# Channel layer norms: the next product takes x shifted by a pivot, and mean and deviation are applied when it is evicted

## What is computed

```python
def layer_norm(x, g, b):
    mu = x32.mean(-1, keepdims=True)
    var = jnp.square(x32 - mu).mean(-1, keepdims=True)
    return ((x32 - mu) * lax.rsqrt(var + LN_EPS) * g + b)

xp = ffn_sublayer(xp, ffn1_w_gu, ffn1_w_down, ln_g[0], ln_b[0])   # layer_norm(ALPHA*x + 0.5*swiglu(x))
qa, ka, va, qr, kr, vr, gr, ga, gb = split_inputs(xp, w_in)
oa = diff_post(diff_attention_prompt(qa, ka, va, lam), ...)
ob = ret_post(retention_prompt(qr, kr, vr), gr)
xp = merge_sublayer(xp, oa, ob, ga, gb, w_pa, w_pb, w_o, ln_g[1], ln_b[1])
xp = ffn_sublayer(xp, ffn2_w_gu, ffn2_w_down, ln_g[2], ln_b[2])
```

## Time and profile before

| | us |
|---|---|
| median of three runs (1946.41 to 1950.22) | 1946.93 |
| span of the profiled execution (the page gives its span, no other time of it) | 1943.7 |
| busy: PE, DVE, ACT, POOL | 1804.9, 778.9, 667.4, 85.2 |

### The profile page before, as it was taken

The page is one execution under the profiler, slowest core; times in us unless marked ns, Lnnn a source line. Parts: engine busy times, 40 slices in busy tenths (PEclk is TensorE's granted clock), DMA queues, the critical chain, the costliest instruction groups (busy, mean ns, idle before and its releaser), DMA issues.

```text
span 1943.7 us, 33105 instructions
## 1 busy us (share of the span) xinstructions
PE 1804.9 (93%) x13247; PEld 1699.9 (87%) x13247; DVE 778.9 (40%) x1081; ACT 667.4 (34%) x899; POOL 85.2 (4%) x113
## 2 busy tenths in 40 slices
PE   6999999998997768999989999999999899999996
PEld 5999999987997537878768999869998799999996
DVE  2333332234223875756663223344345433333123
ACT  3333331124223555666563222124322433332111
POOL 0000000000002420000000000110000000000002
PEclk9999999999997998999989999999999999999998
DMA  4222222230440015767752232062223022222221
GB/s 142 91 90 91 89 84 82 81 108 22 133 133 23 1 51 176 273 228 249 242 169 91 87 98 84 17 215 66 91 91 100 22 86 87 89 90 84 92 97 46
DMA packets 146659, 203.75 MB, mean 105 GB/s; under 512 B 5538, under 2 KB 127330, under 8 KB 146594
## 3 DMA queue, kind: packets, MB, share of 16 engines
q1 hardware_dynamic: 145442, 198.35, 31.4%
q0 software_dynamic: 1152, 4.46, 0.6%
HBM read 191.39 MB, written 11.40 MB: 104 GB/s over the span
## 4 chain that ended last, share of the span: by engine, by line
PE 88%; DVE 4%; ACT 4%; issue 2%; DMA 0%; SPq 0%; POOL 0%; ACTq 0%; POOLq 0%; DVEq 0%
PE ps L297 68%; PE ps L1201 4%; PE ps L1232 3%; PE ps L1187 2%; PE ps L974 1%; PE ps L988 1%; PE ps L614 1%; PE ps L1624 1%; PE ps L1211 1%; PE ps L1616 1%; PE ps L1248 1%; PE ps L699 1%; PE ps L1198 1%; ACT aT L1069 1%; PE ps L981 0%
## 5 line engine op out<-in xcount | busy, mean ns | idle before, releaser
L297 PE MATMUL ps<-xh,w_hi_t 128*128 128x272 f32 x2432 | 510.1, 291 | 25.3 <-DVE xl L651 18.3
L297 PE MATMUL ps<-xh,w_lo_t 128*128 128x272 f32 x2432 | 505.9, 290 | 0.0
L297 PE MATMUL ps<-xl,w_hi_t 128*128 128x272 f32 x2432 | 504.2, 289 | 0.0
L283 DVE TENSOR_TENSOR w_lo_t<-w_raw,w_hi_t 128x2048 fp32r<-128x2048 f32 (+1 forms) x112 | 252.4, 2254 | 519.2 <-ACT w_hi_t L279 519.2
L297 PEld LDWEIGHTS ps<-xh,w_hi_t 128*128 128x128 f32 x2432 | 385.0, 190 | 30.2 <-issue 20.7
L297 PEld LDWEIGHTS ps<-xl,w_hi_t 128*128 128x128 f32 x2432 | 385.1, 190 | 0.0
L297 PEld LDWEIGHTS ps<-xh,w_lo_t 128*128 128x128 f32 x2432 | 382.4, 190 | 0.0
L279 ACT CAST w_hi_t<-w_raw 128x2048 fp32r<-128x2048 f32 (+1 forms) x112 | 209.9, 1874 | 276.5 <-PE ps L297 276.5
L297 PE MATMUL ps<-hh,w_lo_t 128*128 128x272 f32 x704 | 145.7, 288 | 0.0
L297 PE MATMUL ps<-hh,w_hi_t 128*128 128x272 f32 x704 | 145.5, 288 | 0.0
L297 PE MATMUL ps<-hl,w_hi_t 128*128 128x272 f32 x704 | 145.1, 288 | 0.0
(11 more groups left out here) (245 smaller groups left out, 2107.0 us busy)
## 6 DMA issues: line engine op xcount, KB each, us to landing
w_raw<-in_ffn_w_gu_dram SPq DMA_DIRECT2D x44, 1024.0 KB, 5.1
w_raw<-in_w_in_dram SPq DMA_DIRECT2D x32, 1024.0 KB, 5.7
k_page<-in_cache_k_dram SPq DMA_DIRECT2D x64, 512.0 KB, 4.8
v_page<-in_cache_v_dram SPq DMA_DIRECT2D x64, 512.0 KB, 4.6
w_raw<-in_ffn_w_down_dram SPq DMA_DIRECT2D x16, 1024.0 KB, 5.1
w_raw<-in_ffn_w_down_dram SPq DMA_DIRECT2D x8, 768.0 KB, 4.7
w_raw<-in_w_branch_a_dram SPq DMA_DIRECT2D x4, 1024.0 KB, 5.2
st_in<-in_state_ret_dram SPq DMA_DIRECT2D x8, 512.0 KB, 5.0
```

Of the source, the lines that this page charges most:

```text
L283: nc.vector.tensor_tensor(w_lo_t[:, j, 0:nk], w_raw[:, j, 0:nk], w_hi_t[:, j, 0:nk].bitcast(F32), ALU.subtract).then_inc(lo_split, 1)
L297: mm = nc.tensor.matmul(ps[:, bank + half, 0:HALF], w[:, j, k, w_cols], m[:, k0 + k, half * HALF:half * HALF + HALF], start=start and k == ...
```

## The change

What goes into the next product is no longer the normalised x. With a pivot c for each token (the mean of the first 256 channels), x - c is formed early; `xh` and `xl` get g * (x - c), and two more columns, -g and b, stand behind the 544 tokens. The product then holds W'g(x - c) and, in the two columns, -W'g and W'b. Mean and deviation of x - c come later, and the eviction computes (product + mean * (-W'g)) / deviation + W'b, in three DVE instructions (`dve_fix`) and the bias of the ACT instruction that evicts anyway. So:

- **Pivot.** When two of the 8 tiles are done, DVE adds them, PE multiplies by ones (`pe_pivot`, behind the first chunk of the second pair in the down projection and behind tile 2 of the output projection), ACT scales, and DVE adds -c to all 8 tiles of `xT`, the six that still lack their product among them (`dve_pivot`).
- **Each tile** is then squared and multiplied by g on ACT (`act_take`), the squares are added up on POOL in `x_ssq`, and DVE adds `x_sum` and makes the low part. `x_sq` is a single buffer.
- **The sums** over channels of `x_sum` and `x_ssq` are made by PE inside the next product's first tile, between its fifth and sixth k step (`between`, `pe_stats`).
- **Normalised x** is still needed: by the value projection after the first norm and from round 1 on in FFN 2. POOL subtracts the mean, DVE scales, ACT adds the bias and makes `xh`, DVE `xl`, all between the evictions of the product that took the raw x. `xh` is overwritten k by k behind that product's last tile (`freed`).
- `NormedProject` replaces `Project` for the key projection (all 8 tiles on raw x); in FFN 2 only round 0 is on raw x and stands written out ahead of the loop. The loops of the down projections and of the output projection are written out on PE, and on all three engines for the output projection.

The diff, cut to its core:

```diff
-        def gemm(bank, j, n, nk, mh_, ml_, k0=0, start=True, stop=True, tile_ready=None):
+        def gemm(bank, j, n, nk, mh_, ml_, k0=0, start=True, stop=True, tile_ready=None, extra=0, freed=None,
+                 between=None):
             for k in range(nk):
+                if between and k == 5:
+                    between()
                 if tile_ready:
                     tile_ready(k)
                 w_cols = slice(n * P, n * P + P)
                 for pas, (w, m) in enumerate(((w_hi_t, mh_), (w_hi_t, ml_), (w_lo_t, mh_))):
                     for half in range(2):
-                        mm = nc.tensor.matmul(ps[:, bank + half, 0:HALF], w[:, j, k, w_cols],
-                                              m[:, k0 + k, half * HALF:half * HALF + HALF],
+                        cols = HALF + extra * half
+                        mm = nc.tensor.matmul(ps[:, bank + half, 0:cols], w[:, j, k, w_cols],
+                                              m[:, k0 + k, half * HALF:half * HALF + cols],
                                               start=start and k == 0 and pas == 0,
                                               stop=stop and k == nk - 1 and pas == 2)
+                if freed and k < nk - 1:
+                    mm.then_inc(freed, 1)
             mm.then_inc(gemm_done, 1)
         def tile_done(eng, c, n):
...
+            def pe_up(self, pe, i, tile_ready=None, folded=None):
                 c = self.c
-                with pe.Fori(0, KF // 2) as i:
-                    for j in range(2):
-                        chunk_ready(pe, c + 2 * i + j)
-                        for n in range(2):
-
-                            pe.wait_ge(self.prod_done if j else self.silu_done, self.h0 + 2 * i + n + 1)
-                            gemm(4 * j + 2 * n, j, n, KD, xh, xl, tile_ready=None if j or n else tile_ready)
+                for j in range(2):
+                    chunk_ready(pe, c + 2 * i + j)
+                    for n in range(2):
+                        pe.wait_ge(self.prod_done if j else self.silu_done, self.h0 + 2 * i + n + 1)
+                        if folded and j:
+                            folded.sums_read(pe, n)
+                        first = j == 0 and n == 0
+                        gemm(4 * j + 2 * n, j, n, KD, xh, xl, tile_ready=tile_ready if first else None,
+                             extra=2 if folded else 0, freed=folded.freed if folded and j and n else None,
+                             between=(lambda: folded.pe_stats(pe)) if folded and first else None)
...
+                if folded:
+                    self.pe_up(pe, 0, lambda k: folded.raw_ready(pe, k), folded)
+                with pe.Fori(1 if folded else 0, KF // 2) as i:
...
+                for q in range(2):
...
+                                if norm and q == 1 and r == 0 and s == 0 and n == 0:
+                                    norm.pivot_kept(pe)
...
+                            if norm and q == 0 and m == 3:
+                                norm.pe_pivot(pe)
...
+            def dve_up(self, dve, i, folded=None):
                 c = self.c
-                with dve.Fori(0, KF // 2) as i:
-                    split_lo(dve, c + 2 * i + 2, 0)
+                if folded:
                     for n in range(2):
+                        folded.dve_fix(dve, n, c, n, 2 * n)
+                split_lo(dve, c + 2 * i + 2, 0)
+                if folded:
+                    for k in range(KD):
+                        folded.dve_scale(dve, k)
+                for n in range(2):
...
+                    if folded and n == 0:
+                        for k in range(KD):
+                            folded.dve_low(dve, k)
+                split_lo(dve, c + 2 * i + 3, 1)
...
+                ln2.dve_columns(dve)
+                for k in range(KD):
+                    c = self.c + k // 2
+                    tile_done(dve, c, k % 2)
+                    if k > 2:
+                        ln2.dve_shifted(dve)
+                    nc.vector.scalar_tensor_tensor(halves(xT[:, k]), banks(2 * (k % 4)), 1.0 / ALPHA, halves(xT[:, k]),
+                                                   ALU.mult, ALU.add).then_inc(self.resid, 1)
+                    if k == 2:
+                        dve.wait_ge(self.resid, k + 5)
+                        ln2.dve_pivot(dve)
+                        ln2.dve_raw_low(dve, 0)
+                        ln2.dve_raw_low(dve, 1)
+                    ln2.dve_take(dve, k, self.resid, 0)
+                    if k % 2 == 1:
+                        split_lo(dve, c + 2, k // 2 % 2)
+                ln2.dve_stats(dve)
```

More of the change, by code:

```diff
@@ L379, in act_part @@
+            def act_part(self, act, folded=None, norm=None):
+                c = self.c
+                if folded:
+                    self.act_up(act, 0, folded)
+                with act.Fori(1 if folded else 0, KF // 2) as i:
+                    self.act_up(act, i)
                 c += FFN_UP
+                if norm:
+                    norm.act_columns(act)
                 for q in range(2):
@@ L384, in act_part @@
                             split_hi(act, c + nxt, (c + nxt) // 2, m % 2, 6 if m % 3 == 0 else KD)
-            def dve_part(self, dve, norm=None):
+                        if norm and q == 0 and m == 3:
+                            norm.act_pivot(act)
+                            for k in range(2):
+                                norm.act_take(act, k, self.resid, self.r0)
+                        if norm and m % 3 == 2 and (q, m) != (0, 2):
+                            for k in (4 * q + 2 * (m // 3), 4 * q + 2 * (m // 3) + 1):
+                                norm.act_take(act, k, self.resid, self.r0)
@@ L400, in dve_part @@
-                    split_lo(dve, c + 2 * i + 3, 1)
+                    dve.wait_ge(self.h_hi, self.h0 + 2 * i + n + 1)
+                    nc.vector.tensor_tensor(hl[:, bass.ds(2 * i + n, 1)], prod[:, n:n + 1],
+                                            hh[:, bass.ds(2 * i + n, 1)].bitcast(F32),
+                                            ALU.subtract).then_inc(self.h_lo, 1)
+                    if folded and n == 0:
+                        for k in range(KD):
+                            folded.dve_low(dve, k)
@@ L401, in dve_part @@
+                split_lo(dve, c + 2 * i + 3, 1)
+            def dve_part(self, dve, folded=None, norm=None):
+                c = self.c
+                if folded:
+                    self.dve_up(dve, 0, folded)
+                with dve.Fori(1 if folded else 0, KF // 2) as i:
+                    self.dve_up(dve, i)
                 c += FFN_UP
@@ L412, in dve_part @@
                                 k = 4 * q + 2 * r + n
+                                if norm and k >= 2:
+                                    norm.dve_shifted(dve)
                                 nc.vector.scalar_tensor_tensor(halves(xT[:, k]), banks(4 * r + 2 * n), 0.5 / ALPHA,
@@ L1971, in _ @@
             out_proj.act_part(act)
[L1972 to L1973 removed]
+            ffn2.act_part(act, folded=ln2)
             ln3.act_part(act)
```

350 lines of the change are left out of this document (219 added, 131 removed).

## The result

The changed kernel takes 1925.08 us (median of 4 runs, 1923.93 to 1932.02) beside 1948.58 for the kernel before on the same chip: ratio 0.9881, 95% interval 0.986 to 0.9903. That is 23.5 us less, where 34.7 were forecast, and above the top of the range (1922). The profiled span is 1922.8 us after 1943.7: 20.9 less, and 13.8 more than the 1909.0 of the forecast. What follows looks for the 13.8 us.

A forecast was written before the change was run, and what follows sets the result against it. TensorE, 88% of the chain that ended last, was taken as the bound. Stall 55.9 - 6.8 first norm - 11.0 second norm - 3.4 clock = 34.7 us off 1946.93: 1912 us, range 1904 to 1922.

The forecast's parts named there:

- The stall, 55.9 us: TensorE's time lost at the two channel norms: 28.5 us at the first, 27.4 at the second, the most winnable.
- what remains of it: Added TensorE work and waits left after the change: 6.8 us at the first norm, 11.0 at the second.
- The waits: TensorE idle: 2.2 us before the sums' products, 1.6 before first transposes, 2.1 before output-projection tile 6, 5.9 before FFN 2 round 1.
- POOL and DVE exclude one another: Around both norms, a DVE instruction with two SBUF operands and a POOL instruction were taken never to run together.
- Rival 1: POOL and DVE do not hinder each other in the norm stages and the clock falls once: 1907 us, chance 0.22.
- rivals 2, 3 and 4: Stall moves to FFN 2 round 1, 1922; POOL makes DVE the bound, 1949 (0.04); k=5 stop, 1919; 2 and 4 together 0.20.
- The clock: TensorE runs at half pace after the 5.9 us wait and one wait near 2 us: 3.4 us lost.
- Written out or looped, PE keeps one pace: Writing out the down and output projections costs nothing, at 0.125 us a matmul either way.
- the two new columns: Two columns more in half of 576 matmuls: 288 x 2 x 0.46 ns = 0.3 us, neglected.

The follow-up runs named there:

- views: The changed kernel with rows of xh and xl 546 elements apart only while raw x stands there, 544 for all else: 1912.91 us, ratio 0.9817.

## Why the prediction was wrong

*The stall, 55.9 us, and what remains of it:* right. The waits came where they were forecast; they are 2.9 us smaller in sum. The lengths of the steps hold: POOL's addition 1.36 us (I took 1.3), the sums' and squares' products 1.19 and 1.18, the reciprocal 3.55.

*POOL and DVE exclude one another:* right as a mechanism. In the changed kernel the second correction of FFN 2's fix 0 took 1.53 us beside POOL, and 0.72 at 1518.21, in fix 2, when POOL was done:

```profile
1503.49 1.53 DVE L825 TENSOR_TENSOR x_fix<-x_fix,x_rs 128x544 f32<-128x544 f32 x1
```

Rival 1, which had them free of each other, falls with that; rivals 2, 3 and 4 fall with the waits: no wait of 16 us, no path lengthened by 39, no stop of half the stall.

*The clock:* 2.2 us instead of 3.4, one fall.

*The step that failed* is the sentence "Written out or looped, PE keeps one pace", with the neglect of the layout that goes with it. Of written out and looped it is right (both kinds slowed down alike); what does not hold is the pace itself, which the sum took over from the kernel before. I priced the two new columns by their count (0.3 us, right) and did not price what they do to the rows behind them: in the kernel, `xh` and `xl` are now `[KD, T + 2]`, and `xl` starts 64 bytes later. Matmuls on `xh` and `xl` throughout the kernel, not just the 576 with more columns, got slower, by 1.67 ns in FFN 1: 7296 x 1.67 ns = 12.2 us.

The miss in the profile, then: 12.2 of pace, 4.3 of the decoding stage, less 2.9 of shorter waits and 1.2 of clock, together 12.4 of 13.8 us; 1.4 I can't place. The pace is shown by the runs; the 4.3 is a measured length whose cause is open. The test of the account is views, which gives 1.39 of the 1.67 ns back for all but 576 matmuls: ratio 0.9817, 35.6 us of 1946.93, for a forecast of 34.7. That it comes so close is in part luck, since its profile also has the shorter decoding stage (430.2).

## What to carry to other kernels

When a diff changes a tensor's shape or address, list every instruction that reads the tensor, in stages that the change doesn't touch too, and price a nanosecond each: 7296 matmuls make 12 us of 1.7 ns. Look first at a stage ahead of the change: if its pace moved, the new work there can't be the cause, and the layout is the first thing to test alone. Move one thing at a time: here several of the layouts tried also moved the start of `xl`, which has a price of its own. Where odd rows are needed for a short while, give the bytes a second name with the odd distance and keep the aligned one for the rest.
